# A decoder step on one core: page numbers read once for both kinds of cache, and the new values' product with 128 rows

## The chip, the cores and the metric

The kernel runs on one core of a Trainium2 chip. The metric is the device time of one execution in microseconds (us), the median of the runs; lower is better. Before the change it is 2517.35 us (three runs, 2516.94 to 2517.95). Numbers are float32 throughout; large products are made of two rounded parts (`w_hi`, `w_lo`).

## What is computed

One layer of a hybrid decoder, for a prompt of 512 tokens and for 8 sequences of 4 new tokens each, with shared weights. After an RMS norm one projection feeds four token mixers (pooling, a gated recurrence, forgetting attention "FoX", stick-breaking attention "SB"); their outputs are normed per group, mapped by an output projection and added; then comes a squared-ReLU MLP of width 8192. The change touches the attention of the 8 sequences. Each attends to 2048 cached positions, which lie as 16 pages of 128 rows in a pool, and to the 4 new ones:

```python
rows = pool[page_table]                       # gather_pages: 16 page numbers for each sequence
fk_all = jnp.concatenate([past_fox_kv[:, :, 0], fk], axis=1)
fv_all = jnp.concatenate([past_fox_kv[:, :, 1], fv], axis=1)
sk_all = jnp.concatenate([past_sb_kv[:, :, 0], sk], axis=1)
sv_all = jnp.concatenate([past_sb_kv[:, :, 1], sv], axis=1)
# FoX:  softmax(q.k/8 + cq - ck) v      SB:  exp(log_sigmoid(z) + sum of log_sigmoid(-z) behind) v
```

Both kinds of cache are read through the same table, so sequence b uses the same 16 page numbers for FoX and for SB.

## The kernel before, in words

The five engines run one program each (`@block.sync` is SP, then `gpsimd`, `scalar`, `vector`, `tensor`) and meet through semaphores; the order on each engine is the order of the code. SP issues nearly all transfers from one queue. The stages on TensorE (PE) are: the input projection of 36 chunks of weights of 128 x 2048 (to about 468 us), the attention stage (to about 880 us), and the output projection and the MLP (to the end).

**The start.** SP issues the parameters, then in four rounds q = 0..3 a quarter of the input (`x_in`, 1088 KB) and a quarter of the first weight chunk (`w_raw[1]`, 256 KB), with two waits between (L705 to L713). `w_piece_in[0]` tells that the first quarter of the weights has landed, `x_loaded[0]` that the first quarter of the input has. ScalarE rounds each to its high part, VectorE (DVE) makes the low part, and PE multiplies quarter by quarter (`first_products`), with the forget gate's small products (`gate_products`) between.

**The attention stage.** It has 32 prompt units (i, 8 heads x 4 blocks of queries) and 16 sequence units (u), one for every two of the prompt's. Sequence unit u is sequence b = u // 2 and kind x = u % 2: FoX for even u, SB for odd u. In a unit PE makes the scores (`seq_scores`): a mask, the product with the new keys (`k_new`, L2041), then 16 products with the cached keys (L2046). These have 128 rows and write 32 output rows each, four in four column groups of the array. Then ScalarE and DVE make weights of the scores, PE turns them (`seq_turn`), ScalarE copies them to `pt_t` and, for the 32 new tokens, to `pt_new` (`seq_turned`), and PE weighs the values (`seq_weigh`): for each c of 4 four products of 128 rows with `v_ring` (L2086), and ahead of the last four the product with the new values (L2084). This has 32 rows, the 32 new tokens, and writes the output rows 96 to 127, as the fourth of each four does.

**The transfers of the stage.** The keys of a unit are 16 transfers of 256 KB into `k_ring`, which holds one unit, so SP issues those of u + 1 (`load_keys`, L686) when the scores of u are done (`d_score`). The values are another 16 into `v_ring`, which holds one unit too; POOL issues each four when the products of the same four of the unit before are done (`d_av`), in `load_values` (L914). For u = 0 the last eight of the values are issued by SP (L783 to L787). Ahead of the transfers of each unit both engines load the 16 page numbers of its sequence from `ids` into registers (`value_load`, L689 on SP, L912 on POOL), and SP loads eight more at L785. On SP this stands ahead of the wait for `d_score`.

**The hand-over to it.** When the last chunk is done, PE turns the new values (`turn_values`, ten groups), ScalarE copies them from PSUM into `v_tok` and `v_new` (`v_store`, each raises `v_stored`), POOL clears `c_prompt` and `q_pad`, and DVE copies the queries into `q_pad` (`pad_queries`) and makes the running sum `pc`.

## Time and profile before

| what | us |
|---|---|
| median of three runs | 2517.35 |
| the profiled execution | 2517.61 |
| its span, first to last instruction | 2515.5 |
| PE busy | 2479.8 (99%) |
| DVE busy | 1334.0 (53%) |
| ScalarE (ACT) busy | 914.0 (36%) |
| POOL busy | 191.7 (8%) |
| granted clock of PE, mean | 0.997 |

The profiled execution is one of the program's executions, with the hardware profiler on; all rows are of it. Times in it are from the span's start. The span is 2.1 us shorter than the time of the same execution, which holds what lies around the first and last instruction. "Busy" of PE counts matmuls (PE) apart from loads of weights (PEld), which run beside them. An idle stretch of PE costs time; one of another engine only where PE waits for it. In the chain of waits PE has 94% of the span, DVE 2%, transfers 1%.

### The profile page before, as it was taken

What the parts mean: (1) busy time and instruction counts of PE and PEld (TensorE: products, weight loads), DVE (VectorE), ACT (ScalarE), POOL (GpSimd) and SP (SyncE); (2) the same over time, 40 slices, a digit from 0 to 9 for tenths busy, and PEclk for the clock granted to TensorE, in tenths of its full rate; (3) what the DMA queues carried; (4) which work ended last, traced back from release to release, by engine and by line L of the source; (5) the groups of instructions that cost most, each with busy time, mean ns of one, the idle gap of its engine ahead of it and who ended that gap; (6) DMA issues with size and microseconds to landing.
All of it is one profiled execution on the core that took longest, in us unless ns stands there. A gap on an engine that the chain in (4) does not pass through costs nothing.

```text
span 2515.5 us, 41732 instructions
## 1 busy us (share of the span) xinstructions
PE 2479.8 (99%) x16734; PEld 2301.3 (91%) x16734; DVE 1334.0 (53%) x1881; ACT 914.0 (36%) x1584; POOL 191.7 (8%) x314
## 2 busy tenths in 40 slices
PE   8999999899999999999999999999999999999999
PEld 7999999755555599999999999999999999999999
DVE  6354455344444587464564554554554554554556
ACT  6244456333333444232333333332332332332333
POOL 0170000223333200000000000000000000000000
PEclk9999999999999999999999999999999999999999
DMA  6322233699999852222222222222222222222222
GB/s 186 116 95 86 84 102 113 254 338 369 370 359 373 309 204 86 99 84 84 98 87 84 87 96 87 84 86 99 84 84 97 89 84 87 99 84 84 101 84 105
DMA packets 104513, 352.45 MB, mean 140 GB/s; under 512 B 22361, under 2 KB 25050, under 8 KB 80770
## 3 DMA queue, kind: packets, MB, share of 16 engines
q1 hardware_dynamic: 84194, 284.25, 32.1%
q0 software_dynamic: 20128, 65.56, 7.1%
q8 instruction: 132, 2.16, 0.3%
q14 instruction: 59, 0.48, 0.1%
HBM read 337.69 MB, written 12.07 MB: 139 GB/s over the span
## 4 chain that ended last, share of the span: by engine, by line
PE 94%; DVE 2%; DMA 1%; SPq 1%; issue 1%; ACT 0%; ACTq 0%; DVEq 0%
PE bank L473 54%; PE bank L478 27%; PE bank L2111 3%; PE bank L2086 2%; PE bank L2046 2%; PE bank L1988 1%; DMA w_raw<-weights 1%; PE bank L1888 1%; PE bank L2017 1%; PE bank L2094 1%; PE bank L2084 1%; PE bank L2002 1%; DVE d_r L1630 0%; PE bank L1991 0%; DMA k_ring<-sb_k 0%
## 5 line engine op out<-in xcount | busy, mean ns | idle before, releaser
L473 PE MATMUL bank<-x_act,w_hi 128*128 128x364 f32 (+1 forms) x4800 | 1044.6, 328 | 1.8 <-DVE w_lo L464 1.7
L473 PEld LDWEIGHTS bank<-x_act,w_hi 128*128 128x128 f32 x4800 | 762.4, 188 | 3.3 <-DVE w_lo L464 2.0
L473 PE MATMUL bank<-hid,w_hi 128*128 128x364 f32 (+1 forms) x3456 | 721.1, 329 | 1.2 <-DVE hid L567 1.2
L478 PE MATMUL bank<-x_act,w_lo 128*128 128x272 f32 x3200 | 642.1, 287 | 1.6 <-DVE x_act L574 1.6
L562 DVE TENSOR_TENSOR sum_tmp<-sum_tmp,bank 128x544 f32<-128x544 f32 x336 | 241.8, 720 | 685.3 <-ACT sum_tmp L556 685.3
L478 PEld LDWEIGHTS bank<-x_act,w_lo 128*128 128x128 f32 x3200 | 553.8, 188 | 4.8 <-DVE w_lo L1324 2.0
L473 PEld LDWEIGHTS bank<-hid,w_hi 128*128 128x128 f32 x3456 | 556.5, 188 | 1.6 <-issue 1.6
L555 ACT ACTIVATE sum_tmp<-bank 128x184 f32<-128x184 f32 x336 | 108.6, 323 | 1012.6 <-PE bank L473 1012.5
L478 PE MATMUL bank<-hid,w_lo 128*128 128x272 f32 x2304 | 429.5, 287 | 1.1 <-DVE hid L567 1.1
L464 DVE TENSOR_TENSOR w_lo<-w_raw,w_hi 128x2048 fp32r<-128x2048 f32 x171 | 392.0, 2292 | 28.3 <-ACT w_hi L447 28.1
L478 PEld LDWEIGHTS bank<-hid,w_lo 128*128 128x128 f32 x2304 | 379.2, 188 | 1.8 <-DVE hid L567 1.8
L447 ACT ACTIVATE w_hi<-w_raw 128x2048 fp32r<-128x2048 f32 x171 | 328.0, 1918 | 0.9 <-DMA w_raw<-weights 0.9
L1758 DVE TENSOR_TENSOR x_res<-x_res,sum_tmp 128x544 f32<-128x544 f32 x272 | 196.9, 724 | 8.3
L556 ACT ACTIVATE sum_tmp<-bank 128x360 f32<-128x360 f32 x336 | 156.8, 467 | 0.0
L2111 PE MATMUL bank<-proj,wo 128*128 128x272 f32 x512 | 137.3, 400 | 3.0 <-DVE xh L1684 2.0
L562 DVE TENSOR_TENSOR proj<-proj,bank 128x544 f32<-128x544 f32 x36 | 25.9, 720 | 161.8 <-ACT proj L556 161.8
L2111 PEld LDWEIGHTS bank<-proj,wo 128*128 128x128 f32 x512 | 89.3, 190 | 20.0 <-issue 7.3
L926 POOL DMA_DIRECT2D v_ring<-fox_v x120 | 64.5, 537 | 394.0 <-PE bank L473 270.1
L926 POOL DMA_DIRECT2D v_ring<-sb_v x128 | 68.7, 537 | 135.0 <-PE bank L2086 126.4
L555 ACT ACTIVATE proj<-bank 128x184 f32<-128x184 f32 x36 | 11.6, 321 | 158.2 <-PE bank L473 158.2
L2046 PE MATMUL bank<-k_ring,q_pad 128*32 128x512 f32 x512 | 61.0, 608 | 6.6 <-DMA k_ring<-sb_k 6.6
L1576 DVE TENSOR_REDUCE stat<-bank 128x1 f32<-128x128 f32 (+3 forms) x32 | 15.7, 492 | 93.5 <-PE bank L1991 93.5
(247 smaller groups left out, 1488.1 us busy)
## 6 DMA issues: line engine op xcount, KB each, us to landing
w_raw<-weights SPq DMA_DIRECT2D x171, 1024.0 KB, 4.8
k_ring<-fox_k SPq DMA_DIRECT2D x128, 256.0 KB, 7.8
k_ring<-sb_k SPq DMA_DIRECT2D x128, 256.0 KB, 6.9
v_ring<-sb_v POOLq DMA_DIRECT2D x128, 256.0 KB, 5.2
v_ring<-fox_v POOLq DMA_DIRECT2D x120, 256.0 KB, 4.7
wo<-w_early SPq DMA_DIRECT2D x16, 512.0 KB, 9.4
x_in<-xT SPq DMA_DIRECT2D x4, 1088.0 KB, 6.7
kv_out<-proj SPq DMA_DIRECT2D x3, 1088.0 KB, 8.8
```

Source lines behind the costliest of these rows:

```text
L447: nc.scalar.activation(w_hi[c0 % 2][:], w_raw[c0 % 2][:], ACT.Copy).then_inc(w_high, 1)
L464: nc.vector.tensor_tensor(w_lo[c0 % 2][:], w_raw[c0 % 2][:], w_hi[c0 % 2][:].bitcast(F32), ALU.subtract).then_inc(w_low, 1)
L473: ins = nc.tensor.matmul(bank[:, base + b, 0:n], hi, row[:, t:t + n], start=begin, stop=end)
L478: ins = nc.tensor.matmul(bank[:, base + b, 0:HALF], lo, row[:, t:t + HALF], start=False, stop=False)
L555: nc.scalar.activation(out[:, :, 0:EXTRA], bank[0:rows, b:b + 2, HALF:SPAN], ACT.Copy)
L556: nc.scalar.activation(out[:, :, EXTRA:], halves(bank[0:rows, b + 2, 0:2 * THIRD]), ACT.Copy).then_inc(extra, 1)
L562: nc.vector.tensor_tensor(out, out, bank[0:rows, b:b + 2, 0:HALF], ALU.add).then_inc(evac, 1)
L926: pool.dma_start(v_ring[:, n % V_SLOTS, j], (fox_v, sb_v)[x][bass.ds(pages[4 * j + c], 1)].rearrange("a p n -> (a p) n")).then_inc(v_loade ...
L1758: v.tensor_tensor(x_res[:, t], x_res[:, t], sum_tmp[n % 2][:], ALU.add).then_inc(added, 1)
L2046: ins = mm(bank[ROWS * j:ROWS * j + ROWS, 4], q_pad[x][:, b, a], k_ring[:, j, :, a], start=(x == 1 and a == 0), stop=(a == 3))
L2086: ins = mm(bank[ROWS * j:ROWS * j + ROWS, 6], pt_t[:, c, ROWS * j:ROWS * j + ROWS], v_ring[:, (4 * u + c) % V_SLOTS, j], start=(c == 0), s ...
L2111: ins = mm(bank[:, early_bank(i), 0:HALF], wo[t % 2][:, k], y, start=(k == 0), stop=(k == 2 * GT - 1))
```

## The change

1. The page numbers are loaded once for a sequence, at its FoX unit, and kept in registers for the SB unit, on SP and on POOL. SP's eight value transfers for u = 0 use the kept numbers too.
2. The product with the new values has 128 rows. `v_new` and `pt_new` are 128 rows high, their rows 32 to 127 are zeros, and are cleared once: `v_new` by DVE, ahead of its wait for the cleared `q_pad`, `pt_new` by POOL, after the new values' first five groups are turned. ScalarE waits for both before it writes the upper 32 rows. The counts that wait for `c_ready` go up by two. The product's code (L2084) is as it was; the tiles are taller.
3. At the start the two waits of SP change places: the second quarter of the input is issued when the first quarter of the input is in, the third when the first weight piece is.

```diff
@@ -200,7 +200,7 @@
     v_tok = [r.take(f"v_tok{x}", [P, GT, D_GROUP]) for x in range(2)]
     A_Q_PAD = r.next
     q_pad = [r.take(f"q_pad{x}", [P, DEC_BATCH, PAIRS, ROWS]) for x in range(2)]
-    v_new = [r.take(f"v_new{x}", [NEW, D_GROUP]) for x in range(2)]
+    v_new = [r.take(f"v_new{x}", [P, D_GROUP]) for x in range(2)]
     k_new = [r.take(f"k_new{x}", [P, PAIRS, NEW]) for x in range(2)]
     pf = [r.take(f"pf{i}", [P, SEQ]) for i in range(2)]
     pa = [r.take(f"pa{i}", [P, SEQ]) for i in range(2)]
@@ -210,7 +210,7 @@
     ps = [r.take(f"ps{i}", [P, SEQ]) for i in range(2)]
     ptf = r.take("ptf", [P, SEQ])
     pts = r.take("pts", [P, SEQ])
-    pt_new = r.take("pt_new", [NEW, P])
+    pt_new = r.take("pt_new", [P, P])
     r = Region(A_PROJ + SV * SLOT, A_PROJ + (SV + 1) * SLOT)
     d_p = r.take("d_p", [P, PAGE * 4 + NEW])
     d_l = r.take("d_l", [P, PAGE * 4 + NEW])
@@ -683,11 +683,14 @@
 
     @block.sync
     def _(sp):
+        pages = []
+
         def load_keys(u):
             b, x = divmod(u, 2)
 
-            pages = [sp.value_load(ids[0:1, PAGES * b + n:PAGES * b + n + 1], min_val=0, max_val=POOL_PAGES - 1)
-                     for n in range(PAGES)]
+            if x == 0:
+                pages[:] = [sp.value_load(ids[0:1, PAGES * b + n:PAGES * b + n + 1], min_val=0, max_val=POOL_PAGES - 1)
+                            for n in range(PAGES)]
             if u >= 1:
                 sp.wait_ge(d_score, u)
             for j in ((1, 0, 2, 3) if u == 0 else range(4)):
@@ -704,9 +707,9 @@
         for q in range(4):
 
             if q == 1:
+                sp.wait_ge(x_loaded[0], 16)
+            if q == 2:
                 sp.wait_ge(w_piece_in[0], 16)
-            if q == 2:
-                sp.wait_ge(x_loaded[0], 16)
             sp.dma_start(x_in[:, 4 * q:4 * q + 4], xT[:, 4 * q:4 * q + 4]).then_inc(x_loaded[q], 16)
             if q == 0:
                 sp.dma_start(w_raw[0][:, 0:KT * ROWS], w_forget).then_inc(w_loaded[0], 16)
@@ -782,8 +785,7 @@
 
         for c in (2, 3):
             for j in range(4):
-                page = sp.value_load(ids[0:1, 4 * j + c:4 * j + c + 1], min_val=0, max_val=POOL_PAGES - 1)
-                sp.dma_start(v_ring[:, c, j], fox_v[bass.ds(page, 1)].rearrange("a p n -> (a p) n")
+                sp.dma_start(v_ring[:, c, j], fox_v[bass.ds(pages[4 * j + c], 1)].rearrange("a p n -> (a p) n")
                              ).then_inc(v_first[c - 2], 16)
         for u in range(2 * DEC_BATCH):
             if u + 1 < 2 * DEC_BATCH:
@@ -800,7 +802,7 @@
 
         sp.wait_ge(v_loaded[3], 64 * (2 * DEC_BATCH - 1))
         sp.dma_start(sv_prompt, v_tok[1][:]).then_inc(kv_stored, 16)
-        sp.dma_start(sv_new, v_new[1][:]).then_inc(kv_stored, 16)
+        sp.dma_start(sv_new, v_new[1][0:NEW]).then_inc(kv_stored, 16)
         for s in range(X_SLOTS):
             sp.wait_ge(xh_stored[s], 16 * ((STORED.index(LATE[0]) - 1 - s) // X_SLOTS + 1))
         sp.wait_ge(kv_stored, 16 * 3)
@@ -907,14 +909,14 @@
                                          bass.IndirectOffsetOnAxis(ap=idx[:, j:j + 1], axis=0)).then_inc(lf_gather, 16)
         pool.wait_ge(lf_gather, 16 * 9)
         pool.sem_inc(lf_rows, 1)
-        def page_numbers(b):
-
-            return [pool.value_load(ids[0:1, PAGES * b + n:PAGES * b + n + 1], min_val=0, max_val=POOL_PAGES - 1)
-                    for n in range(PAGES)]
+        pages = []
 
         def load_values(u):
             b, x = divmod(u, 2)
-            pages = page_numbers(b)
+
+            if x == 0:
+                pages[:] = [pool.value_load(ids[0:1, PAGES * b + n:PAGES * b + n + 1], min_val=0, max_val=POOL_PAGES - 1)
+                            for n in range(PAGES)]
             for c in range(4) if u else (0, 1):
                 n = 4 * u + c
                 if n >= V_SLOTS:
@@ -935,6 +937,9 @@
             own.then(nc.gpsimd.memset(q_pad[x][:], 0.0))
         own.wait()
         pool.sem_inc(q_cleared, 1)
+
+        pool.wait_ge(v_turned, 5)
+        nc.gpsimd.memset(pt_new[:], 0.0).then_inc(q_cleared, 1)
         for u in range(1, 2 * DEC_BATCH):
             load_values(u)
         end_stage(pool, 1)
@@ -1094,12 +1099,13 @@
             if tt < 4:
                 f(v_tok[x][:, tt], bank[:, turn_bank(n)], ACT.Copy).then_inc(v_stored, 1)
             else:
-                f(v_new[x][:], bank[0:NEW, turn_bank(n)], ACT.Copy).then_inc(v_stored, 1)
+                act.wait_ge(c_ready, x + 1)
+                f(v_new[x][0:NEW], bank[0:NEW, turn_bank(n)], ACT.Copy).then_inc(v_stored, 1)
 
         for n in range(10):
             v_store(n)
         act.wait_ge(q_cleared, 1)
-        act.wait_ge(c_ready, 1)
+        act.wait_ge(c_ready, 3)
         f(c_prompt[0:HEADS], pc[0:HEADS], ACT.Copy).then_inc(v_stored, 1)
         nc.scalar.preload_act_table_set("natural_log_exp_and_others")
         act.wait_ge(kv_stored, 16 * 3)
@@ -1168,8 +1174,10 @@
             act.wait_ge(d_pt, u + 1)
             if u >= 1:
                 act.wait_ge(d_av, 4 * u)
+            if u == 0:
+                act.wait_ge(q_cleared, 3)
             own.then(f(pt_t[:], bank[:, 5].rearrange("p (j r) -> p j r", j=4), ACT.Copy))
-            f(pt_new[:], bank[0:NEW, 6, 2 * P:3 * P], ACT.Copy).then_inc(d_ptsb, 1)
+            f(pt_new[0:NEW], bank[0:NEW, 6, 2 * P:3 * P], ACT.Copy).then_inc(d_ptsb, 1)
 
         def seq_weight(u):
             act.wait_ge(d_shift, u + 1)
@@ -1546,6 +1554,9 @@
         dve.wait_ge(strips, 4 * C_OUT)
         dve.wait_ge(head_norm, 8)
         dve.wait_ge(q_scaled, 1)
+
+        for x in range(2):
+            v.memset(v_new[x][:], 0.0).then_inc(c_ready, 1)
         dve.wait_ge(q_cleared, 2)
 
         def pad_queries(x):
@@ -1562,7 +1573,7 @@
         v.tensor_tensor_scan(pc[0:HEADS], ones[0:HEADS, 0:1].to_broadcast([HEADS, SEQ]), logit[:, 0:SEQ], 0.0,
                              ALU.mult, ALU.subtract).then_inc(c_ready, 1)
         pad_queries(1)
-        dve.wait_ge(c_ready, 1)
+        dve.wait_ge(c_ready, 3)
 
         dve.wait_ge(v_stored, 11)
         v.tensor_tensor(c_prompt[HEAD_DIM:], pc[0:HEADS], c_prompt[0:HEADS].bitcast(F32), ALU.subtract).then_inc(c_ready, 1)
@@ -2119,7 +2130,7 @@
                 seq_scores(u)
             if i == 0:
                 pe.wait_ge(v_stored, 10)
-                pe.wait_ge(c_ready, 2)
+                pe.wait_ge(c_ready, 4)
             if not odd and u >= 1:
                 seq_combine(u - 1)
             early_product(i, 0)
```

On SP, from the last of u = 0's value transfers of SP (`v_ring<-fox_v`) to the first keys of u = 1 (`k_ring<-sb_k`), before (register moves are not among the rows; an ISA row computes an address or checks a bound):

```order
L785 TENSOR_LOAD ids
L785 ISA x2
L786 ISA
L786 DMA v_ring<-fox_v 128x512
L689 TENSOR_LOAD ids
L689 ISA x2
...
L699 ISA [waits d_score]
L699 DMA k_ring<-sb_k 128x512
```

and now:

```order
L762 DMA dconst<-dconsts 128x1412 [waits strips]
L771 DMA wo_125<-w_early 128x1024 [waits y_normed,head_norm]
L771 DMA wo_126<-w_early 128x1024
L788 DMA v_ring<-fox_v 128x512 x8
L702 DMA k_ring<-sb_k 128x512 [waits d_score]
L702 DMA k_ring<-sb_k 128x512 x15
L692 TENSOR_LOAD ids
```

Eight loads between the value transfers and 16 between them and the keys are gone; the next loads stand behind the keys, for u = 2.

On DVE, where the attention stage begins (`q_pad` takes the queries), before:

```order
L562 TENSOR_TENSOR proj<-proj,bank 128x544 [waits extra]
L1343 TENSOR_TENSOR proj<-proj,x_rs 128x544 [waits evac]
L1557 COPY q_pad_115<-proj 64x8x4 [waits head_norm,q_scaled,strips,q_cleared,lru_states,scaled]
L1557 COPY q_pad_115<-proj 64x8x4 x7
L1558 COPY k_new_119<-proj 128x128
```

and now:

```order
L562 TENSOR_TENSOR proj<-proj,bank 128x544 [waits extra]
L1351 TENSOR_TENSOR proj<-proj,x_rs 128x544 [waits evac]
L1559 MEMSET v_new_117 128x512 [waits head_norm,strips,q_scaled,lru_states,scaled]
L1559 MEMSET v_new_118 128x512
L1568 COPY q_pad_115<-proj 64x8x4 [waits q_cleared]
L1568 COPY q_pad_115<-proj 64x8x4 x7
```

Two memsets stand where DVE waited for POOL (`q_cleared`).

## Rows read from the trace of the kernel before

**Rows 1.** The page's busy shares, and a stretch by engine with clock and transfers.
```profile
PE 2479.8 (99%) x16734; PEld 2301.3 (91%) x16734; DVE 1334.0 (53%) x1881; ACT 914.0 (36%) x1584; POOL 191.7 (8%) x314
...
560.00:800.00 240.00, 235.34 (x1659) 136.72 (x1660) 108.78 (x284) 80.91 (x231) 78.22 (x146) 1.00 0.99 369
```

**Rows 2.** Waits of PE and of SP: total us, times, longest.
```profile
PE bank L2046 <- DMA k_ring<-sb_k: 6.6, 1, 6.6
...
SPq L699 <- PE bank L2046: 76.4, 14, 7.6
```

**Rows 3.** Timeline of SP (start, us), and its page-number loads from 470 to 486.
```profile
467.40 8.32 SPq L786 DMA_DIRECT2D v_ring<-fox_v  x8
...
L689 SPq TENSOR_LOAD <-ids x16: 262/266/273, 475.8 to 484.0; - x16
...
484.71 8.56 SPq L699 DMA_DIRECT2D k_ring<-sb_k  x16
```

**Rows 4.** Timeline of PE, key products of u = 0 and of u = 1.
```profile
474.81 0.63 PE L2046 MATMUL bank<-k_ring,q_pad 128*32 128x512 f32 x3
474.83 0.26 PE L2041 MATMUL bank<-k_new,q_pad 128*32 128x32 f32 x3
...
474.93 3.60 PE L2046 MATMUL bank<-k_ring,q_pad 128*32 128x512 f32 x29
...
502.75 5.27 PE L2046 MATMUL bank<-k_ring,q_pad 128*32 128x512 f32 x32 [6.59 <-DMA k_ring<-sb_k]
```

**Rows 5.** From issue to landing, the 16 key transfers of u = 1.
```profile
DMA to landing us min/median/max: 2.7/5.3/9.7
```

**Rows 6.** The stretch of PE's wait (columns of Rows 1's second row).
```profile
499.30:502.70 3.40, 0.00 (x0) 0.00 (x0) 0.00 (x0) 0.00 (x0) 2.27 (x5) 0.50 1.04 418
```

**Rows 7.** Timeline of PE, the value products of u = 0.
```profile
490.70 2.78 PE L2086 MATMUL bank<-v_ring,pt_t 128*32 128x512 f32 x24
493.41 1.04 PE L2084 MATMUL bank<-v_new,pt_new 32*32 32x512 f32 x2
494.38 1.07 PE L2086 MATMUL bank<-v_ring,pt_t 128*32 128x512 f32 x8
495.38 0.35 PE L2034 MATMUL bank<-dconst,const 128*96 128x32 f32 x2
```

**Rows 8.** The hand-over: DVE's first copy, and POOL's memsets (ns min/median/max).
```profile
470.82 0.91 DVE L1557 COPY q_pad<-proj 64x32 f32<-64x32 f32 x8 [0.31 <-POOLq L937]
...
L935 POOL MEMSET q_pad<- x2: 946/948/950, 468.8 to 469.7; 128x1024 f32 x2
```

**Rows 9.** The start: SP's issues, the first one's landing, and PE.
```profile
1.34 0.42 SPq L710 DMA_DIRECT2D x_in<-xT  x1
...
7.89 0.33 SPq L710 DMA_DIRECT2D x_in<-xT  x1
...
DMA to landing us min/median/max: 5.3/5.3/5.3
...
29.76 0.43 PE L473 MATMUL bank<-x_act,w_hi 128*128 128x364 f32 x1 [1.70 <-DVE w_lo L464]
```

**Rows 10.** Last key transfer of u = 15 and u = 13: issue, landing, first product.
```profile
L699 SPq DMA_DIRECT2D k_ring<-sb_k x1: 377/377/377, 842.5 to 842.5; - x1
...
DMA to landing us min/median/max: 9.6/9.6/9.6
...
852.20 0.59 PE L2046 MATMUL bank<-k_ring,q_pad 128*32 128x512 f32 x1
...
L699 SPq DMA_DIRECT2D k_ring<-sb_k x1: 333/333/333, 791.1 to 791.1; - x1
...
DMA to landing us min/median/max: 8.7/8.7/8.7
...
802.43 0.63 PE L2046 MATMUL bank<-k_ring,q_pad 128*32 128x512 f32 x3
```

**Rows 11.** A stretch behind the attention stage (columns of Rows 1).
```profile
888.50:895.10 6.60, 6.04 (x23) 5.57 (x22) 6.18 (x13) 2.63 (x4) 0.00 (x0) 0.50 1.00 381
```

## The prediction, on record before the run

> **What bounds the kernel now.** I read the busy shares first. TensorE (PE) is busy for 2479.8 of 2515.5 us [rows 1], so nothing off PE's path can be worth more than the 35.7 us in which it is not, plus what makes its own work slow. Then I read the list of waits for PE: one wait stands out, 6.6 us, once, in the key products (L2046) for a transfer into k_ring of the second kind [rows 2]. Third came the timeline of SP and PE around that wait [rows 3, 4], and then the stretches with their granted clock. The reader is to see that the attention stage (about 470 to 880) is paced by PE, with the DMA engines close behind: share 0.99 and 369 GB/s from 560 to 800 [rows 1]. That nearness decides how much of a gain is kept, so I come back to it in the rivals.
>
> **Part 1, page numbers read once.** The sequence kinds alternate, u = 0 FoX, u = 1 stick-breaking, and so on, 16 units in all. After the keys of u = 0 SP issues eight value transfers with a load of a page number ahead of each: 8.32 us for eight [rows 3], and then 16 more loads (L689) from 475.8 to 484.0, before it can even look at its semaphore. Only then does it issue the keys of u = 1, at 484.71 [rows 3]. What it waits for was long there: the first key products start at 474.81 and the last 29 records run from 474.93 for 3.60 us, so the scores were done at 478.5 [rows 4]. Their 16 issues take 8.56 us [rows 3], the last is out at 492.9, and the longest landing of the 16 is 9.7 us [rows 5]: 502.6 for the last, and PE resumed at 502.75 after 6.59 us of idling [rows 4]. Without the 24 loads SP is through with the value transfers at about 471 and issues the keys at about 478.7, 6.0 us earlier. With the issues as long as now they end near 487.3. The landing moves by more than 6.0: the last transfers now land late (9.7 us, median of the 16 5.3 [rows 5]) because POOL's value transfers, which the first value products release, are beside them; the moved ones land before those begin. So the last lands at 487.3 + 5.3 = 492.6 at the median, and at 497.0 at the worst (9.7). PE is ready at 502.75 - 6.59 = 496.16. Taken: the wait goes whole, **-6.6**; bounds -5.7 (the worst landing) and -6.6.
>
> In the wait the granted clock falls: it is 0.50 (the lower of the two levels, 1.2 GHz) from 499.30 to 502.70 with PE idle [rows 6], and the key products behind it take 5.27 us for 32 records [rows 4], against 3.72 at full clock (474.81 to 474.93 + 3.60). No idling, no fall: **-1.55**; bounds 0 (the clock falls anyway) and -1.55.
>
> At every other unit the loads are hidden: behind them SP still waits for PE's scores, 14 times and 76.4 us in all [rows 2], and POOL waits for the value products in the same way. There the removal is worth 0, and as nothing is added, it can't cost anything either.
>
> **Part 2, the product of 128 rows.** At the end of each unit PE weighs the values: 24 records of 128*32 from 490.70, the new values' product as two records of 32*32 from 493.41, 8 records of 128*32 from 494.38, and the next work at 495.38 [rows 7]. Each record set of eight costs (2.71 - 1.00) / 2 = 0.855 us (24 records take 2.71, 8 take 1.00, the difference is 16), so a switch of form costs 1.00 - 0.855 = 0.145 us behind, and 0.97 - 0.855 = 0.115 us in front. The row count costs nothing: with one switch each, the two records with 32 rows take 0.97 us and a set with 128 rows 1.00. After the change it has the form of its neighbours and writes the same 32 output rows as the last of each four, so it stays in series with that one but not with the other three. Products of one such column group run beside the next ones' other groups already now: L2046 starts at 474.81 while L2041's last three records start at 474.83 [rows 4]. The chain through that column group is three plus one plus one sets, 5 x 0.855 + 0.145 = 4.42, against 495.38 - 490.70 = 4.68 now: 0.25 less. Fifteen units so, and half of it in the last, where PE does transposes ahead of the product: **-3.9**. Bounds 0 (it drains all the same) and -4.2.
>
> The Trainium skill's "TensorEngine Tiling (Array Packing)", When to Use Tiling, speaks against this edit: a contract dimension of 32 should be row-tiled four ways. Its Key Properties add that a change of mode drains the engine. By the first rule the 32-row form is the good one and the edit gives nothing or a loss; by the rows, nothing else fills the other three row groups there and both forms stream alike, so the sum with the first rule would be 3.9 us worse.
>
> **Part 3, the hand-over.** The zeros must be written. DVE gets two memsets of 128x512 ahead of the padding copies that start at 470.82 [rows 8]. The trace has none on DVE of that size; POOL's of 128x1024 takes 948 ns [rows 8], so 0.47 us each for half of it as the upper end; the lower is 0, if both fit in the 0.31 us that DVE stands idle there. ScalarE's copy of v_new now waits for the first memset, and the later copies into v_tok run behind it; PE's first mask product follows the eighth of these copies without a pause, so a delay of them can reach PE. Between 0 and +0.5; taken **+0.2**. POOL's memset of pt_new follows at about 470.7 and is read at 488: nothing. The reader c_ready >= 4 stands ahead of PE's work at 478, three us after it is met: nothing.
>
> **Part 4, the start.** SP issues the second x_in when the first weight piece is in, at 7.89. The first x_in was issued at 1.34 and landed 5.3 us later, at 6.6 [rows 9]. With the two waits exchanged the second x_in goes out 1.25 us earlier. The DMA engines have nothing else then, and everything from there to PE's restart at 29.76 (behind a wait of 1.70 for w_lo [rows 9]) hangs on this stream or on work that starts from it. Taken **-1.2**; bounds 0 (DVE's work becomes the bound) and -1.3.
>
> **One thing is late next.** The keys of the last unit were issued at 842.5 and landed 9.6 us later, 852.1; the product started at 852.20 [rows 10]. The period and the way from the weighing to the scores both shorten by 0.25, so keys are needed 0.5 earlier than now, relative to what releases them: **+0.4** there. Elsewhere they land in time: for the unit at 802.43 at 791.1 + 8.7 = 799.8 [rows 10], 2.6 us ahead.
>
> **Sum.** -6.6 - 1.55 - 3.9 + 0.2 - 1.2 + 0.4 = -12.65. The profiled execution took 2517.61 us (span 2515.5, and 2.1 around it), 0.3 over the runs' median of 2517.35. 2517.6 - 12.65 = **2505.0**.
>
> **Rivals.**
> *The transfers pace the stage.* If the DMA engines have no room, PE keeps only the 6.0 us by which the stream starts earlier, and the 3.9 and the clock go into waits for keys: 1.2 + 6.0 - 0.2 = 7.0, **2510.6**. For it: share 0.99. Against: from 502.75 to 852.20 a unit takes 349.45 / 14 = 24.96 us, at 369 GB/s 9.2 MB; the engines reach 418 [rows 6], at which that takes 22.0, and PE never waited for keys but once. The Trainium skill's "DMA: Bandwidth & Descriptors", Issuing engines are not separate DMA queues, bears it out in part: SP's and POOL's transfers share the same engines. Chance 0.12.
>
> *The throttle at 888 goes or moves.* From 888.50 to 895.10 the clock is 0.50 with PE busy 6.04 us [rows 11]. If the new timing avoids it, up to half of these come back, 3.0: **2502.0**. Against: what PE does before it is unchanged. Chance 0.08. The Trainium skill's "TensorE: Matmul & The Clock Gate", What's actually happening, says that the monitor does not start anew with the kernel, so that the point of a change varies; no row here shows such a shift, the three runs lie within 1.0 us.
>
> *The key wait stays.* The loads go but the landing is held by something else (the 9.7 us): -3.9 - 1.2 + 0.2 = -4.9, **2512.7**. Chance 0.06.
>
> *Slower: keys late at every unit.* With PE and SP nearer together the keys of a unit queue behind the values before them. The place is the wait ahead of L2046, in each of 14 units. They have 2.6 us in hand, 2.1 after the change; each us beyond costs 14. From 2.1 + 12.65 / 14 = 3.0 us later the kernel is slower than before; at 3.5 it is 14 x 1.4 - 12.65 = +7, **2524.5**. For it: the last unit has nothing in hand even now. Against: bytes and releases are the same. Chance 0.03.
>
> My forecast has 0.71. **The range**: 2500.8 to 2510.8 reaches over the first two rivals and the bounds of parts 1 to 4. A difference of 0.2% (5 us) is what a measurement tells from none. Faster by more: the forecast, the first two rivals and a third of the third, which is at the edge, 0.93; within 0.04, slower 0.03.
>
> **What would show it.** SP issues k_ring<-sb_k near 477.5 on the new profile's axis and PE's list has no key wait over 1 us before the last unit; the stretch around 499 has clock 1.00; the new values' product is 128*32, and the value products to the next work take 4.4 us; PE's restart near 28.5. Wrong it is if PE waits for keys in most units, if the product's sets still stand apart, or if the clock falls at a new place.

## The result, and the profile after

The changed kernel takes 2503.63 us (median of 5 runs, 2503.31 to 2503.85), the kernel before 2517.35 (5 runs beside them). The ratio is 0.9945, 95% interval 0.9932 to 0.9959: 13.7 us less. A second set of five runs gave 2503.57 (0.9948, 0.9934 to 0.9962). The forecast was 2505.0, 1.4 us more, with a sum of -12.65.

The busy shares and the stretch from 560 to 800 of the kernel after, with the columns of [rows 1]. A row of a stretch has its start and end, its length, the busy time (and count) of PE, PEld, DVE, ACT and POOL, then the granted clock (0.50 is the lower level, called half clock below), the share of the DMA engines and GB/s:

```profile
PE 2472.8 (99%) x16734; PEld 2302.7 (92%) x16734; DVE 1334.8 (53%) x1883; ACT 913.9 (37%) x1584; POOL 189.4 (8%) x315
...
560.00:800.00 240.00, 236.27 (x1696) 139.65 (x1695) 104.88 (x275) 80.51 (x231) 85.21 (x160) 1.00 0.99 370
```

PE has the same 16734 products and is busy 7.0 us less: part of the gain is idle time that went, part is work that runs faster. The share of the DMA engines is 0.99 as before; it told nothing of a limit.

The keys of u = 1, timelines of SP and PE and the landing (the answers to [rows 3 to 5]; L702 is L699 of before, L2057 is L2046, L2052 is L2041):

```profile
465.63 3.80 SPq L788 DMA_DIRECT2D v_ring<-fox_v  x8
477.82 8.05 SPq L702 DMA_DIRECT2D k_ring<-sb_k  x16
...
DMA to landing us min/median/max: 2.6/5.0/6.0
```

```profile
494.89 0.63 PE L2057 MATMUL bank<-k_ring,q_pad 128*32 128x512 f32 x3
494.92 0.26 PE L2052 MATMUL bank<-k_new,q_pad 128*32 128x32 f32 x3
495.01 3.60 PE L2057 MATMUL bank<-k_ring,q_pad 128*32 128x512 f32 x29
```

SP waits for the scores again and issues the keys the moment they are done; no transfer takes more than 6.0 us to land, and the product starts without a wait. Two stretches by the granted clock. The first holds the key products of u = 1, which ran at half clock before; the second is the same work as in [rows 11], 12.6 us earlier:

```profile
495.00:498.60 3.60, 3.60 (x39) 1.45 (x33) 0.19 (x1) 0.00 (x0) 3.36 (x8) 1.00 0.95 349
...
875.88:882.48 6.60, 5.75 (x37) 5.13 (x36) 6.18 (x13) 2.63 (x4) 0.00 (x0) 1.00 1.00 385
```

Both stretches of half clock are gone. The value products of u = 0 ([rows 7]; L2097 weighs the cached values, L2095 the new ones):

```profile
489.96 3.20 PE L2097 MATMUL bank<-v_ring,pt_t 128*32 128x512 f32 x27
492.58 0.59 PE L2095 MATMUL bank<-v_new,pt_new 128*32 128x512 f32 x1
492.99 0.60 PE L2097 MATMUL bank<-v_ring,pt_t 128*32 128x512 f32 x3
493.01 0.59 PE L2095 MATMUL bank<-v_new,pt_new 128*32 128x512 f32 x1
493.44 1.02 PE L2097 MATMUL bank<-v_ring,pt_t 128*32 128x512 f32 x2
494.39 0.35 PE L2045 MATMUL bank<-dconst,const 128*96 128x32 f32 x2
```

From 489.96 to 494.39 it is 4.43 us for 4.68, and the new values' product now lies between its neighbours. The hand-over ([rows 8]), ScalarE and PE:

```profile
470.13 0.59 ACT L953 ACTIVATE v_new<-bank 32x512 f32<-32x512 f32 x1 [0.30 <-DVE v_new L1559]
...
472.26 0.33 PE L2045 MATMUL bank<-dconst,const 128*96 128x32 f32 x2 [0.36 <-ACT v_tok L953]
```

The start ([rows 9]) and the last unit's first key product ([rows 10]):

```profile
6.67 0.33 SPq L713 DMA_DIRECT2D x_in<-xT  x1
```

```profile
28.65 0.77 PE L473 MATMUL bank<-x_act,w_hi 128*128 128x364 f32 x3 [1.48 <-DVE w_lo L464]
...
839.74 1.50 PE L2057 MATMUL bank<-k_ring,q_pad 128*32 128x512 f32 x12 [0.29 <-DMA k_ring<-sb_k]
```

### The profile page after: what moved, and what is told of

Its sections match the earlier page's. It is cut to its first block, busy times and chain, and to the rows that moved or that the text cites. A ratio compares the mean times of both kernels' runs of the same rounds, so it can differ in the third digit from the quotient of the medians.

```text
span 2501.9 us, 40689 instructions
## 1 busy us (share of the span) xinstructions
PE 2472.8 (99%) x16734; PEld 2302.7 (92%) x16734; DVE 1334.8 (53%) x1883; ACT 913.9 (37%) x1584; POOL 189.4 (8%) x315
## 4 chain that ended last, share of the span: by engine, by line
PE 94%; DVE 3%; DMA 1%; issue 1%; ACT 1%; SPq 0%; ACTq 0%; DVEq 0%
PE bank L473 54%; PE bank L478 27%; PE bank L2122 3%; PE bank L2097 3%; PE bank L2057 2%; PE bank L1999 1%; DMA w_raw<-weights 1%; PE bank L1899 1%; PE bank L2028 1%; PE bank L2105 1%; PE bank L2013 1%; DMA k_ring<-sb_k 0%; DVE d_r L1641 0%; PE bank L2002 0%; SPq L702 0%
## 5 line engine op out<-in xcount | busy, mean ns | idle before, releaser
L2097 PE MATMUL bank<-v_ring,pt_t 128*32 128x512 f32 x512 | 72.4, 596 | 0.0
L555 ACT ACTIVATE proj<-bank 128x184 f32<-128x184 f32 x36 | 11.6, 322 | 158.1 <-PE bank L473 158.1
```

The lines of the kernel that those rows point to most:

```text
L555: nc.scalar.activation(out[:, :, 0:EXTRA], bank[0:rows, b:b + 2, HALF:SPAN], ACT.Copy)
L2097: ins = mm(bank[ROWS * j:ROWS * j + ROWS, 6], pt_t[:, c, ROWS * j:ROWS * j + ROWS], v_ring[:, (4 * u + c) % V_SLOTS, j], start=(c == 0), s ...
```

## The experiments

The medians of one kernel differ by up to about 1 us, so the terms are read from the traces, and the medians say whether their sum stands. First each part by itself on the kernel before.

**Part 1 alone**: the page numbers kept from the FoX unit, on SP and POOL.

```diff
-            pages = [sp.value_load(...) for n in range(PAGES)]
+            if x == 0:
+                pages[:] = [sp.value_load(...) for n in range(PAGES)]
...
+ (the same on POOL, and SP's eight value transfers use pages[4 * j + c])
```

> The kernel before with the page numbers read once alone, on SP and on POOL; product and start as before. Theory (terms add): the key wait of 6.6 us goes and with it the half clock around 500, worth 1.55: -8.15, 2509.2 us, and 0.3 to 0.5 us may go into key waits at the last unit. SP issues the keys of u = 1 at about 479, PE has no key wait over 1 us before the last unit. Rival (the transfers pace the stage): only the 6.0 us by which the stream starts earlier are kept, 2511.4, and key waits appear at later units. Rival (the half clock near 888 goes with whatever shortens the stage): the profile has no stretch of 0.50 near 880 and the time is 1 us less than by the theory, about 2508.2. By the theory that stretch is still there, since PE's work before it is unchanged.

Measured: 2508.49 us, ratio 0.9966 (0.9953 to 0.9978). Timelines of SP and PE, units 1, 2 and 15:

```profile
478.79 8.84 SPq L702 DMA_DIRECT2D k_ring<-sb_k  x16
```

```profile
496.10 0.63 PE L2048 MATMUL bank<-k_ring,q_pad 128*32 128x512 f32 x3
...
522.36 0.63 PE L2048 MATMUL bank<-k_ring,q_pad 128*32 128x512 f32 x3
...
844.00 0.64 PE L2048 MATMUL bank<-k_ring,q_pad 128*32 128x512 f32 x4
```

From the first key product of u = 1 to that of u = 2 it is 26.26 us, for 27.81 before (502.75 to 530.56): 1.55, the clock's term. From u = 2 to u = 15 it is 321.64, and before 321.64 (530.56 to 852.20): seven more sets of page numbers gone on each of SP and POOL, and nothing gained, as for hidden loads. The half clock at 888 is gone too, against the theory and with its rival.

**Part 1 without "once for both"**: only SP's eight value transfers of u = 0 use numbers that are already in registers.

```diff
+            if u == 0:
+                first[:] = pages
...
-                page = sp.value_load(ids[0:1, 4 * j + c:4 * j + c + 1], min_val=0, max_val=POOL_PAGES - 1)
-                sp.dma_start(v_ring[:, c, j], fox_v[bass.ds(page, 1)]...
+                sp.dma_start(v_ring[:, c, j], fox_v[bass.ds(first[4 * j + c], 1)]...
```

> The kernel before with one line of part 1: SP's eight value transfers of u = 0 use the page numbers that SP had loaded for the keys of u = 0 (kept in registers); all 16 loads ahead of every unit's keys stay, and POOL is as before. Theory: what made the keys of u = 1 late was the sum of 8 and 16 loads. The value transfers then take 3.8 us for 8.3, the 16 loads end at about 479.5, just when the scores are done, and the keys go out within 1 us of the time that they have in the kernel with all of part 1: -8.15, 2509.2 us, at least -7.5. So reading once for both kinds, which the change is named after, is worth nothing by itself. Rival (each load counts): the keys are issued only 4.5 us earlier, a wait of about 2 us is left: -4.5 to -6, 2512. The other units' loads are hidden by both.

Measured: 2508.88 us, 0.9963 (0.995 to 0.9977).

```profile
468.61 3.70 SPq L789 DMA_DIRECT2D v_ring<-fox_v  x8
481.61 8.62 SPq L703 DMA_DIRECT2D k_ring<-sb_k  x16
```

The keys go out 1.2 us after the scores are done at 480.39, where all of part 1 has them out at once, and PE has no key wait at u = 1. (The theory had them within 1 us; the keys land 1.7 us before PE needs them, so it makes no difference.) Eight removed loads do what 24 on SP, and all on POOL, do: the theory holds, and the edit that the change is named after was needed for none of it.

**Part 2 and 3 alone**: the product of 128 rows with its memsets and waits (the diff is the change's own).

> The kernel before with the 128-row product alone (zeros in v_new and pt_new, memsets and waits with it); page numbers and start as before. Theory: 0.25 us for each of 15 units and 0.12 for the last, -3.9, and +0.4 for the hand-over's memsets: -3.5, 2513.9 us. The key wait at u = 1 grows by the 0.25 us that PE is there earlier, so that -3.2 is the lower end. Rival (transfers or SP pace the stage, the saved time goes into key waits): less than 1 us faster, 2516.5, with more key waits in the list. Rival (row count costs): the product takes no less than the two switches did, no change in the time from the first value product to the next work (4.68 us).

Measured: 2513.58 us, 0.9987 (0.9978 to 0.9996), 3.6 us less.

```profile
491.25 3.20 PE L2095 MATMUL bank<-v_ring,pt_t 128*32 128x512 f32 x27
...
495.67 0.35 PE L2043 MATMUL bank<-dconst,const 128*96 128x32 f32 x2
...
501.55 5.96 PE L2055 MATMUL bank<-k_ring,q_pad 128*32 128x512 f32 x32 [5.09 <-DMA k_ring<-sb_k]
```

The value products take 4.42 us. The DMA share from 560 to 800 is 1.00 and the saved time was kept: from the first key product of u = 2 to that of u = 15 it is 318.89 us for 321.64, which is 13 times 0.25 less 0.5 that went into the last unit's keys. So the transfers do not pace the stage. The key wait did not grow but shrank to 5.1. Of these 1.5 us only 0.3 come from PE, which is ready later because of the hand-over (496.46 for 496.16); the other 1.2 come from the keys, which in this profile landed 8.5 us after their last issue, for 9.7 before. Why they landed sooner is not shown. In exchange the key products, which now began earlier, took 5.96 us, mostly at half clock. That trade returns below.

**What in the product counts**: 64 rows of the 128, with everything else as after.

```diff
-  mm(bank[3 * ROWS:, 6], pt_new[:, 3 * ROWS:], v_new[x][:], start=False, stop=False)
+  mm(bank[3 * ROWS:, 6], pt_new[0:2 * NEW, 3 * ROWS:], v_new[x][0:2 * NEW], start=False, stop=False)
```

> The changed kernel with 64 of the 128 rows in the new values' product (form 64*32; rows 0 to 63 of v_new and pt_new; the result is the same). Theory (what 128 rows gain is that the product has its neighbours' form): with 64 rows both switches come back, the value products to the next work take 4.68 us for 4.43 in every unit, +3.9, 2507.5 us. Rival (what cost was the tile of 32 rows itself, its smaller slice of the array): 64 rows keep half of the gain or all of it, +2 or 0, 2505.5 or 2503.6.

Measured: 2507.87 us, 0.9966 (0.9954 to 0.9978), 4.2 above the changed kernel.

```profile
489.63 2.78 PE L2097 MATMUL bank<-v_ring,pt_t 128*32 128x512 f32 x24
492.34 1.04 PE L2095 MATMUL bank<-v_new,pt_new 64*32 64x512 f32 x2
493.31 1.07 PE L2097 MATMUL bank<-v_ring,pt_t 128*32 128x512 f32 x8
494.31 0.35 PE L2045 MATMUL bank<-dconst,const 128*96 128x32 f32 x2
```

4.68 us again, to the hundredth what 32 rows took [rows 7]. What costs is not the number of rows but a form other than the neighbours'.

**The chain through one column group**: the product cut into four column groups.

```diff
-  mm(bank[3 * ROWS:, 6], pt_new[:, 3 * ROWS:], v_new[x][:], start=False, stop=False)
+  for j in range(4):
+      f = slice(P * j, P * j + P)
+      mm(bank[ROWS * j:ROWS * j + ROWS, 6, f], pt_new[:, 3 * ROWS:], v_new[x][:, f], start=False, stop=False)
```

> The changed kernel with the new values' product cut into four of 128 columns, one in each column group (output rows 0 to 31, 32 to 63, ...), for one of 512 columns in the last group. The output is not the reference's, since each group's rows are weighted with that group's own weight afterwards and the new values' part needs the last one's; the work is the same in size. Theory (what the product costs is the chain of five sets through one column group, 5 x 0.855 + 0.145): now each group has four sets and a quarter, 4.25 x 0.855 + 0.145 = 3.78 us for 4.43 from the first value product to the next work, 0.64 less in 16 units, -10.3, 2493.3 us; some of it, up to 1 us, may go into the last unit's key wait. Rival (the transfers pace the stage from here on): the value products shorten as said, but the keys of the odd units, which have 2.2 to 2.5 us in hand, come late after a few units and PE waits for them; the stage gives back 0 to 3 us, 2501 to 2503.6. Rival (the array takes the groups' products one after the other there): no less than 4.3 us, 2503.6 or more.

Measured: 2495.05 us, 0.9915 (0.9901 to 0.9929).

```profile
489.97 2.78 PE L2100 MATMUL bank<-v_ring,pt_t 128*32 128x512 f32 x24
492.57 0.40 PE L2097 MATMUL bank<-v_new,pt_new 128*32 128x128 f32 x8
492.79 1.04 PE L2100 MATMUL bank<-v_ring,pt_t 128*32 128x512 f32 x8
493.76 0.35 PE L2045 MATMUL bank<-dconst,const 128*96 128x32 f32 x2
...
833.63 4.95 PE L2057 MATMUL bank<-k_ring,q_pad 128*32 128x512 f32 x32 [3.81 <-DMA k_ring<-sb_k]
```

3.79 us for 3.78 by the chain of four and a quarter sets: the model of the prediction holds. Of the 10.3 us 8.6 reach the median. What is missing is in the last unit: its keys are late, 3.8 us of wait here for 0.3, and the clock falls in it, so that its key products take 4.95 us for 3.64. These 4.8 us are nearly all that the profiled execution (2498.5 us) lacks to the forecast; the median lacks less. From u = 2 to u = 13 (519.62 to 781.64) a unit takes 23.82 us for 24.46, so there nothing was lost, though the keys land only 0.4 to 3.5 us ahead of their products. This kernel adds the new values' part under other weights than the reference's, so it only shows the size of the prize.

**How late keys may be**: SP issues them 4.5 us later in every unit.

```diff
             if u >= 1:
                 sp.wait_ge(d_score, u)
+                for n in range(8):
+                    sp.value_load(ids[0:1, PAGES * b + n:PAGES * b + n + 1], min_val=0, max_val=POOL_PAGES - 1)
```

> The changed kernel with 8 page-number loads (results unused) behind SP's wait for the scores, ahead of the first key transfer of every unit u >= 1. By SP's eight value transfers, 8.32 us with a load each and 3.80 without, a load costs 0.57 us, so the keys go out 4.5 us later in every unit. This sizes the rival 'keys late at every unit'. As the prediction priced it (all 14 units have 2.1 us in hand, each us beyond costs 14): 14 x 2.4 = +34, 2537 us. Theory now (the keys of odd units have 2.2 to 2.5 us in hand and those of the last none, the even ones mostly 4.1 to 5.0, so only the odd ones wait): 6 x 2.2 + 1.1 + 4.5 = +19, 2522 us. Rival (the landing is set by the engines' backlog and not by the issue): under +5, 2508 us.

Measured: 2508.16 us, 0.9963 (0.995 to 0.9976), 4.5 above the changed kernel. The landings of u = 3's keys, first in this kernel, then in the changed one:

```profile
L704 SPq DMA_DIRECT2D k_ring<-sb_k x16: 346/390/636, 534.2 to 542.2; - x16
...
DMA to landing us min/median/max: 2.7/5.4/6.5
```

```profile
L702 SPq DMA_DIRECT2D k_ring<-sb_k x16: 333/382/480, 524.6 to 532.5; - x16
...
DMA to landing us min/median/max: 6.1/7.2/9.2
```

And the waits for keys:

```profile
PE bank L2059 <- DMA k_ring<-sb_k: 3.7, 3, 3.0
...
498.32 5.34 PE L2059 MATMUL bank<-k_ring,q_pad 128*32 128x512 f32 x32 [2.96 <-DMA k_ring<-sb_k]
```

Both theories that multiplied by the units fall, the one made after the result as well as the prediction's; the third holds. The slowest key transfer of u = 3, issued 4.5 us later, landed 2.7 us sooner after its issue (6.5 for 9.2). That what it stood behind had been moved by then is the likely reason, but not shown by itself. Of the rest the units' reserve, the 2.2 to 5.0 us by which the keys of u = 2 to 14 land ahead of their first product in the changed kernel, takes nearly all: from u = 2 to u = 15 it is 319.42 us for 318.84. Only u = 1 waits for long (3.0). Its keys had nothing beside them and now fall among POOL's values: issued 5.0 us later (482.83 for 477.82), the last landed 6.7 later (498.18 for 491.47). And half clock comes back there: 5.34 us of key products for 3.72. The profiled execution (2510.25) is 6.6 us above that of the changed kernel and not 4.5: 4.8 of them are at u = 1, 0.6 from u = 2 to u = 15, and 1.0 is a fall of the clock behind the attention stage, of which more below.

**The start alone**, on the kernel before:

```diff
             if q == 1:
-                sp.wait_ge(w_piece_in[0], 16)
+                sp.wait_ge(x_loaded[0], 16)
             if q == 2:
-                sp.wait_ge(x_loaded[0], 16)
+                sp.wait_ge(w_piece_in[0], 16)
```

> The kernel before with the two waits at the start exchanged alone. Theory: PE restarts its first products 1.1 us earlier (28.65 for 29.76) and everything behind follows: -1.1, 2516.2 us; the granted clock reaches its upper level at 13.2 us and not at 11.2 as in the kernel before, because of this edit. Rival: the gain at the start is lost at a later wait for a transfer, and the time is unchanged, 2517.35. Rival: the later rise of the clock has another cause, and this kernel's clock is up at 11.2; then the start is worth up to 1.3.

Measured: 2516.86 us, 0.9996 (0.9987 to 1.0005).

```profile
28.39 0.77 PE L473 MATMUL bank<-x_act,w_hi 128*128 128x364 f32 x3 [1.86 <-DVE w_lo L464]
...
501.82 5.74 PE L2046 MATMUL bank<-k_ring,q_pad 128*32 128x512 f32 x32 [7.06 <-DMA k_ring<-sb_k]
```

PE is 1.4 us ahead at 28.39 and still at 474. At the key wait 0.9 of it is left (501.82 for 502.75), because the last landing takes 10.0 us for 9.7; and as the clock rises at the same time as before, 506.1, the key products, which begin earlier, have more of the slow stretch: 5.74 us for 5.27. Behind them 0.5 us is left, and 0.2 behind the keys of the last unit, which land 9.9 us after their last issue for 9.6. So in this profile nearly nothing of the gain arrives. The medians alone can't tell: their interval is -3.3 to +1.3 us and holds -1.1 too. Is the gain kept in the changed kernel, where wait and half clock are gone? The waits of the start put back, twice:

> The changed kernel with the two waits at the start as they were before. Alone, the exchange was worth -0.3 us (ratio 0.9996, 0.9987 to 1.0005), where PE's restart moved by 1.1 to 1.4. Theory (the start's gain was swallowed by the key wait at 502 and the half clock that ends at 506 whatever PE does): with both gone the exchange is worth its full 1.1, so this kernel takes 2503.6 + 1.1 = 2504.7 us, and PE's first key product of u = 1 comes at 496.0 for 494.9. Rival (the start is worth nothing at the end, what it gains is lost in the input projection): 2503.6, and the key product at 494.9.

Measured: 2504.76 us, 0.9956 (0.9942 to 0.9969). The first key product of u = 1 comes at 496.71, later than both forecasts, as PE restarts at 30.49 in this profile. The profiled execution took 2507.27 us, and its last unit shows why:

```profile
843.36 3.64 PE L2057 MATMUL bank<-k_ring,q_pad 128*32 128x512 f32 x32 [2.12 <-DMA k_ring<-sb_k]
```

The keys of u = 15 landed 11.6 us after their last issue, and PE waited 2.1 us for them, for 0.3 in the changed kernel. What these keys cost differs from profile to profile. And the old start beside the changed kernel on one chip:

> The changed kernel once more, on the chip of the two below, so that differences of about 1 us can be read on one chip. By its first runs: 2503.6 us, ratio 0.9945. It has no half clock near 500 and 880 in its profile if these stretches hang on how the work lies in time and are the same from run to run; if they come and go by chance, one may be there.

> The changed kernel with the two waits at the start as before, once more and beside the changed kernel. Theory (the exchange is worth its 1.1 us only where no key wait at 502 swallows it): 1.1 us above the changed kernel of the same chip. Rival (it is worth nothing): the same time.

Measured: 2503.57 and 2505.16 us (0.9953, 0.9939 to 0.9966). The same PE products, first with the new start, then with the old one:

```profile
28.48 0.76 PE L473 MATMUL bank<-x_act,w_hi 128*128 128x364 f32 x3 [1.49 <-DVE w_lo L464]
...
494.71 0.63 PE L2057 MATMUL bank<-k_ring,q_pad 128*32 128x512 f32 x3
```

```profile
30.12 0.77 PE L473 MATMUL bank<-x_act,w_hi 128*128 128x364 f32 x3 [2.18 <-DVE w_lo L464]
...
496.35 0.63 PE L2057 MATMUL bank<-k_ring,q_pad 128*32 128x512 f32 x3
```

1.64 us at the start are 1.64 at 494 and 1.6 at the end (spans 2501.8 and 2503.4). The medians' intervals overlap; it is the traces that show it. All 13 profiles agree on the start: with the old one PE restarts at 29.76 to 30.49 (six profiles), with the new one at 28.33 to 28.85 (seven), 1.5 us earlier in the mean. In the changed kernel this gain reaches the end; that it is lost on the kernel before rests on the one profile above.

**The hand-over**: POOL clears `v_new` in place of DVE.

```diff
+        nc.gpsimd.memset(v_new[0][:], 0.0).then_inc(q_cleared, 1)
         nc.gpsimd.memset(c_prompt[:].bitcast(F32), 0.0).then_inc(q_cleared, 1)
...
+        nc.gpsimd.memset(v_new[1][:], 0.0).then_inc(q_cleared, 1)
...
-        for x in range(2):
-            v.memset(v_new[x][:], 0.0).then_inc(c_ready, 1)
...
-                act.wait_ge(c_ready, x + 1)
+                act.wait_ge(q_cleared, 3 * x + 1)
```

> The changed kernel with v_new cleared by POOL, its first half ahead of c_prompt and q_pad and its second behind them, in place of DVE's two memsets; the waits follow. Theory (the hand-over costs 0.4 us because ScalarE's copy of v_new waits 0.30 us for DVE's memset, and all later copies and PE's mask product run behind it): the wait goes, PE's mask product of u = 0 comes 0.3 to 0.4 us earlier, 0.3 us less in all. Rival (POOL's memset of 128x512, 0.47 us by half of the one of 128x1024, pushes q_pad back and DVE's padding and the key products with it): nothing gained, or up to 0.5 us lost.

Measured: 2503.64 us, 0.9944 (0.993 to 0.9957), no difference that a median shows. ScalarE and PE:

```profile
471.30 0.58 ACT L955 ACTIVATE v_new<-bank 32x512 f32<-32x512 f32 x1
```

```profile
468.62 2.34 PE L1969 MATMUL bank<-const,proj 128*128 128x128 f32 x20
...
473.54 0.33 PE L2044 MATMUL bank<-dconst,const 128*96 128x32 f32 x2
```

Both waits are gone: from the first turned values to the mask product it is 4.92 us, in the changed kernel 5.27 (466.99 to 472.26), before 4.88 (468.11 to 472.99). The 0.35 us are there: the first key product follows the first turned values after 6.72 us for 7.08, and from it to the end both kernels take 2027.9 us. A median is too coarse for it. In this profile the clock fell once near the start, which costs more than that:

```profile
29.30:32.60 3.30, 3.30 (x15) 3.30 (x14) 1.88 (x1) 3.30 (x4) 0.00 (x0) 0.50 0.86 303
```

From PE's restart to the first turned values it is 439.9 us here and in the kernel with the eight loads gone, which has such a fall too, and 438.3 in the other eleven profiles: the fall costs 1.55 us.

## Why the prediction was right

Each term by the two traces:

| term | forecast | measured |
|---|---|---|
| key wait of u = 1 | -6.6 | -6.87 |
| half clock in and behind it | -1.55 | -1.55 |
| product of 128 rows | -3.9 | -3.91 |
| hand-over | +0.2 | +0.38 |
| start | -1.2 | -1.12 |
| keys of the last unit | +0.4 | +0.45 |
| half clock near 888 | 0 | -0.94 |
| sum | -12.65 | -13.56 |

The first six terms sum to -12.62, almost what was forecast. Part of that is luck: the key wait gave 0.27 more, the hand-over cost 0.18 more.

*Key wait.* From the first key product of u = 0 to that of u = 1: 27.94 us before, 20.82 after. Of the 7.12, 0.25 is the product's. The other 6.87 are 0.27 more than the wait: without it the key products begin beside the last of `k_new`'s (494.89 and 494.92) and not behind them. The landing was forecast from the median of before with 9.7 as the worst; it was 6.0 at most, which fits the reason given (no value transfers beside them); the late keys, which do fall among POOL's values, landed 7.5 us after their last issue. But value transfers are not all of it, as the 8.5 us of part 2 alone show. That the loads elsewhere are worth nothing is shown by part 1 alone. But of the 24 loads on SP the eight were enough; the prediction summed them and did not ask which were needed.

*Product.* 4.43 us for 4.42 forecast, in each of 15 units, and 0.16 in the last (from its value products to L641, 12.79 us for 12.95). The Trainium skill's rule in "TensorEngine Tiling (Array Packing)", When to Use Tiling, by which a contract dimension of 32 is for row tiling, would have had the sum 3.9 us worse. For a lone product between others of full height the runs decide against it: 32 and 64 rows took 4.68 us, 128 rows 4.43. The drain at a change of mode, which its Key Properties state, agrees with the 0.25 us that two changes of form cost here.

*Hand-over.* The term was mis-sized: 0.38 for 0.2. Two memsets take 1.03 us, ScalarE waits 0.30 for the first, and PE's mask product comes 0.39 later after the first turned values (5.27 us for 4.88). With POOL's memsets in their place this went, so it is the cause.

*Start.* SP issued the second quarter of the input 1.22 us earlier (6.67 for 7.89) and PE restarted 1.11 earlier, as forecast. Over all profiles it is 1.5, a little beyond the bound of 1.3, so the near match is partly luck.

*Last unit.* From the first key product of u = 14 to that of u = 15 it is 23.75 us, where 0.25 off the 23.51 of before would be 23.26: about 0.5 late. The size is as forecast, the way is not. Measured from the first key product of u = 14, PE needs the keys of u = 15 only 0.25 us earlier, not 0.5, and their last transfer landed 0.24 later (23.61 us for 23.37). In the other profiles this landing scatters by more than that, up to the wait of 2.1 us above, so the match is luck.

*Half clock near 888.* This is what the forecast lacks, and most of what it missed by. The rival that it goes had 0.08 and "up to 3.0". It went here, in both parts done alone and with the eight loads, but not with the start alone. The price was wrong the other way: 1.0 us and not 3. From L641, the first product behind the attention stage, to the end it is 1634.3 us with it (881.24 to 2515.5) and 1633.3 without (868.62 to 2501.9). In the stretch itself DVE is busy 6.18 of 6.60 us in 13 instructions, with the clock at 0.50 [rows 11] as at 1.00. Counted from L641, the kernel before is 2.3 us behind the changed one at the end of its slow stretch, and only 0.94 from 890 on (times of the changed kernel). Most of what it gets back it gets where the changed kernel waits 0.85 us for DVE's sums and it does not (889.03); the changed kernel also waits longer in the stretch itself, 0.85 us for 0.56 (877.09):

```profile
877.09 0.52 PE L478 MATMUL bank<-hid,w_lo 128*128 128x272 f32 x2 [0.85 <-DVE hid L567]
...
889.03 0.74 PE L473 MATMUL bank<-hid,w_hi 128*128 128x364 f32 x3 [0.85 <-DVE sum_tmp L562]
```

When it falls stays open. Besides before and the start alone, three kernels have it at the same place in the work, 6.9 to 7.2 us behind L641 (before 7.2): the one with late keys (L641 7.0 us earlier than before) in full, the one with 64 rows (9.5 us earlier) and the cut product (17.8) for half as long, where it cost nothing (1633.3 us to the end in both). The other eight profiles do not have it. The late keys' kernel, which takes 1634.3 us from L641 (874.22) to the end:

```profile
881.40:888.00 6.60, 6.03 (x23) 5.55 (x22) 6.18 (x13) 2.63 (x4) 0.00 (x0) 0.50 1.00 395
```

The reason given, that what PE does before it is unchanged, was no reason: the same work with and without the fall stands in these profiles.

*The rivals.* "The transfers pace the stage" fell twice: 0.25 and then 0.64 us less per unit were kept up to the last unit, at a share of 0.99 to 1.01. It is right in one place, the last unit, where the keys land 11.5 us after their last issue with the cut product. "The key wait stays" fell. "Slower: keys late at every unit" was priced far too high: 4.5 us of delay should have cost over 30 by its working and cost 4.5, since keys that are issued later land sooner after their issue, and the reserves differ from unit to unit.

## What to carry to other kernels

Ask of a removed wait not only how long it is but what it swallows: a gain ahead of it may be worth little until it is gone (the start: 1.4 us at the restart became 0.2 behind the attention stage when alone, and 1.6 stayed 1.6 with the rest). Of a series of instructions that makes something late, take away only as many as reach the next real wait; here eight loads did the work of all. And where a small product stands between large ones, give it their form, and look at the chain through its part of the array: its rows cost nothing, the change to its form and back 0.25 us each time.

## What the runs showed of the hardware

Half clock came with each of the five waits of 3.0 to 7.1 us in the attention stage (before, the product alone, the start alone, the late keys, the cut product) and not with the wait of 2.1 there; its price lies in the products behind the wait, 1.3 to 2.2 us. It also came near 888 with PE busy, and near 30 in two profiles, behind a wait of 2.0 or 2.1 us. Others have longer waits there without it (2.18 and 2.33 in the two with the old start put back):

```profile
30.40:33.70 3.30, 3.30 (x14) 3.30 (x14) 1.63 (x1) 3.30 (x4) 0.00 (x0) 0.50 0.76 268
```

This is the kernel with the eight loads gone: 14 products in 3.3 us. The changed kernel's second set has 25 in 29.30 to 32.60, at clock 1.00. A profile with such a fall can't be compared with one without it before its 1.55 us are taken off.
